# Layer C: two of the three channel slots run ahead of the gate's projection on TensorE

## What is computed

```python
h = rms_norm(x, rms_g)
z, xbc, dt = _split(h @ w_in, SPLIT_C)                 # gate, channels, steps
xbc, new_conv = causal_conv(xbc, conv_state, conv_w, conv_b)
xs, Bm, Cm = _split(silu(xbc), ...)
y, S = ssd_scan(xs, Bm, Cm, dt, A, S0)                 # chunked scan with a carried state
y = y + d_skip * xs
y = rms_norm(y * silu(z), g_y)                         # per group of 512
return x + y @ w_out
```

## Time and profile before

| | before |
|---|---|
| median of 3 runs (lowest, highest) | 2977.31 us (2972.36, 2978.59) |
| the profiled execution | 2970.96 us, its span 2969.1 us |
| TensorE matmul busy | 2774.0 us, 93% |
| TensorE weight load busy | 2313.0 us, 78% |
| VectorE busy | 1768.1 us, 60% |
| ScalarE busy | 1306.0 us, 44% |
| mean granted clock of TensorE | 0.966 |
| DMA | 324.89 MB, 109 GB/s over the span |

### The profile page before, as it was taken

One profiled execution on the slowest core, in us unless ns is written; L12 is line 12 of the kernel. 1 busy time (PEld: TensorE's weight loads), 2 busy tenths in 40 slices (PEclk: granted clock), 3 DMA queues, 4 the chain that ended last, 5 costly groups with the idle time before them and its releaser, 6 DMA issues. The chain is left out here.

```text
span 2969.1 us, 44869 instructions
## 1 busy us (share of the span) xinstructions
PE 2774.0 (93%) x16154; PEld 2313.0 (78%) x16154; DVE 1768.1 (60%) x4144; ACT 1306.0 (44%) x2635; POOL 45.6 (2%) x165
## 2 busy tenths in 40 slices
PE   6999997899999995799999999899999999599999
PEld 3788986577777774688877888688877888478787
DVE  3344443545555553588887888878887888632322
ACT  4455554534444442355454445544454544411211
POOL 0000000100000000000000000000000000000000
PEclk9999999999999997899999999899999999799999
DMA  5222222423233223633344333333343332244343
GB/s 187 88 91 90 76 76 75 136 92 113 105 116 116 106 90 104 174 91 93 93 122 113 100 100 104 123 112 100 99 122 117 100 99 72 86 167 145 133 143 105
DMA packets 281128, 324.89 MB, mean 109 GB/s; under 512 B 52807, under 2 KB 208970, under 8 KB 276778
## 3 DMA queue, kind: packets, MB, share of 16 engines
q1 hardware_dynamic: 279010, 317.77, 33.8%
q10 hardware_dynamic: 1992, 5.48, 0.5%
HBM read 238.89 MB, written 84.30 MB: 109 GB/s over the span
## 5 line engine op out<-in xcount | busy, mean ns | idle before, releaser
L2157 PE MATMUL bank<-h_high,wx_high 128*128 128x256 f32 (+1 forms) x1536 | 463.1, 301 | 2.3 <-DVE wx_low L2067 2.1
L2157 PE MATMUL bank<-h_high,wx_low 128*128 128x256 f32 (+1 forms) x1536 | 438.0, 285 | 0.0
L2157 PE MATMUL bank<-h_low,wx_high 128*128 128x256 f32 (+1 forms) x1536 | 437.2, 285 | 0.0
L2157 PEld LDWEIGHTS bank<-h_high,wx_high 128*128 128x128 f32 x1536 | 293.6, 191 | 24.5 <-issue 17.1
L2157 PEld LDWEIGHTS bank<-h_high,wx_low 128*128 128x128 f32 x1536 | 293.4, 191 | 17.2 <-issue 14.7
L2157 PEld LDWEIGHTS bank<-h_low,wx_high 128*128 128x128 f32 x1536 | 292.6, 191 | 0.0
L1978 DVE SCALAR_TENSOR_TENSOR conv_acc<-u,convw,conv_acc 128x256 f32<-128x256 f32 (+1 forms) x576 | 246.9, 483 | 13.4 <-ACT conv_acc L1860 11.1
L2148 PE MATMUL bank<-wz_high,h_high 128*128 128x512 f32 (+1 forms) x544 | 224.8, 413 | 5.4 <-DVE wz_low L2072 4.6
L2409 PE MATMUL bank<-wout_high,yT_high 128*128 128x512 f32 (+1 forms) x544 | 213.0, 392 | 6.5 <-DVE wout_low L2378 6.5
L2148 PE MATMUL bank<-wz_low,h_high 128*128 128x512 f32 (+1 forms) x544 | 216.3, 398 | 0.0
L2148 PE MATMUL bank<-wz_high,h_low 128*128 128x512 f32 (+1 forms) x544 | 216.2, 397 | 0.0
(11 more groups left out here) (294 smaller groups left out, 6141.7 us busy)
## 6 DMA issues: line engine op xcount, KB each, us to landing
h_high<-h1T_high_d SPq DMA_DIRECT2D x64, 512.0 KB, 6.1
h_low<-h1T_low_d SPq DMA_DIRECT2D x64, 512.0 KB, 7.0
acb<-acT SPq DMA_DIRECT2D x64, 512.0 KB, 3.8
yT_in<-yT SPq DMA_DIRECT2D x32, 1024.0 KB, 5.1
yT<-yT_t SPq DMA_DIRECT2D x64, 256.0 KB, 3.5
xin<-in_x_prompt SPq DMA_DIRECT2D x16, 512.0 KB, 3.6
h0T_high_d<-hT_high SPq DMA_DIRECT2D x16, 512.0 KB, 2.7
h0T_low_d<-hT_low SPq DMA_DIRECT2D x16, 512.0 KB, 3.5
```

Of the source, the lines that this page charges most:

```text
L2157: ins = M(out, wt[:, k, col:col + P], y[h.par][:, k, h.h0:h.h0 + h.n], start=(k == 0 and p == 0), stop=(k == KT - 1 and p == 2))
```

## The change

The two calls at the head of TensorE's step change places: slots 0 and 1 of the half come first, the gate's projection second. No instruction is added, removed or altered, and no other engine's program changes. In the functions `start` and in steps in which no half is due (the sample's, and units 15 and 16 of the last group) the order stays.

```diff
                 h = nxt.half if nxt is not None and not cur.sample else None
+                if h is not None:
+                    channels(h, cur, 0)
                 if nxt is not None:
                     gate(nxt, cur)
-                if h is not None:
-                    channels(h, cur, 0)
 
                 pe.wait_ge(s["st_new"], cur.st_before)
```

## The result

Six runs of the changed kernel gave a median of 2998.84 us (2991.61 to 3006.16), six of the kernel before 2976.63 us (2969.18 to 2978.59). The ratio is 1.0081, with a 95% interval of 1.0060 to 1.0102: the change makes the kernel slower, by 18 to 30 us. The profiled execution took 3001.40 us, its span 2999.5; against the profiled execution of before that is +30.4 us. That execution of before lay low in its runs and this one lies somewhat above its median, so the traces show 8 us more between them than the medians do.

A forecast was written before the change was run, and what follows sets the result against it. TensorE, busy 93% of the span, was taken as the bound, so time is won or lost where it waits. Terms -9.4 + 14 + 1 + 9 + 14 = +28.6 us, laid on the median, gave 3006 us, range 2979 to 3037.

The forecast's parts named there:

- The gain at the gate: TensorE no longer waits for zs at the gate; the whole excess of 52 units goes, -9.4 us.
- the 52 like units: Units 2 to 14 of each group, 987.5 us together, forecast to fall to 52 x 18.81 = 978.1 us.
- Even units 2 to 12: Late dtk stalls L2227 by 0.7 us in units 4 to 12, +14 us; unit 2 adds +1.
- T: Moment at which TensorE can start the next step: 0.85 us after the start of the state's update.
- VectorE's 2.1 us to spare: In even units, idle time with which VectorE can take back part of the decays' 2.8 us delay.
- the 12.4 us: Typical time from an odd unit's first load to dtk's landing, taken as set by the transfers.
- Rival B: Loads don't matter: VectorE's spare time swallows the delay or transfers land early; 2962 to 2968 us; chance 0.10.
- Unit 14: Unit 13's two more tiles' parts delay dtk; a stall of 3.1 us, 3 x 3 = +9 us.
- rival D: Stalls in units 14 and 16 and paced slots of unit 15 halve the clock: +70 to +85 us; chance 0.07.
- Change of group: In units 15 and 16, late gate weights make unit 16 end 4.6 us later, three times: +14 us.
- the piece that I had put into the range: In unit 15, slots paced by wx_low bring the clock down; second slot and gate pay 2 to 3 us.
- The sum of the terms: Whole kernel: -9.4 + 14 + 1 + 9 + 14 = +28.6 us; end to end +6 to +60.

The follow-up runs named there:

- the run with acb ahead: Changed kernel, but in odd units 1 to 13 SyncE issues store, acb and dtk before the wait for z_full and the pair's loads; 2980.42 us, ratio 1.0020.

## Why the prediction was right

The forecast was 3006 us with 2979 to 3037 around it, on a base of 2977.31; measured were 2998.84. Point by point:

- **The gain at the gate**, -9.4 us: with the loads out of the way the 52 like units fell from 987.5 to 977.8 us, -9.7. Right, and it is all of it: 18.8 us is TensorE's own work in a unit. The reading that 40.9 us of a weight load's idle time are worth 9.4 on TensorE was the step that mattered most on this side.
- **Even units 2 to 12**, forecast +15 with unit 2: the changed kernel has 11.2 us more there than the run with acb ahead, 10.9 of them in units 4 to 12. Landing was forecast at 11.8 to 13.3 us behind the first load; 24 sets of four loads gave 11.1 to 12.8, the three sets of six in unit 13 gave 13.9, 15.0 and 14.9. Decays started at T + 3.7 to 5.6, forecast 4 to 6. VectorE's 2.1 us to spare held: in units 4 to 12 the decays were 2.6 us late on average and the units 0.55 longer.
- **Luck in that landing.** I took the 12.4 us for the time of the transfers, which moves along with the first load. In the kernel before it was not: there the store's wait for VectorE set the issue of dtk, at T + 14.3 on average in units 3 to 11, 8.3 behind the first load, and dtk took 4.4. In the changed kernel the loads set it, at T + 18.6, 7.1 behind the first load, and dtk took 5.1. The two changes nearly cancel, 12.7 against 12.1. Of the 4.9 us by which dtk lands later, 4.3 are a later issue.
- **The order of landing.** dtk landed 1.6 to 3.2 us behind the last load in all 27, never ahead of it. The Trainium skill, page "DMA: Bandwidth & Descriptors", section "Queues, rings and completion order", has both halves, ring order and completion that is not first-in-first-out. These landings do not contradict the first, but they hardly test it: dtk was also issued 6.5 to 9.9 us behind the first load. Rival B fell with the measured time and with these landings; what held dtk up was chiefly that SyncE issues in order.
- **Unit 14**, forecast +9: 11.2. The three units grew by 3.1, 4.9 and 3.2 us where 3.1 was worked out, but not all of that is the wait: TensorE waited at L2187 and L2227 for 1.9, 2.9 and 2.7 us. In groups 0 and 1 the clock went down after it: from the start of L2227 to the next T took 3.7 and 4.3 us in place of 2.6. That is the term of the sum that was too small, by 2 us, for a clock that I had put into rival D alone.
- **Change of group**, forecast +14: unit 16 +18.6, unit 15 -3.8, together +14.8. Unit 16 was forecast to grow by 6 and grew by 5.2, 6.7 and 6.7. Unit 15 was forecast at 25.4 and took 27.0, 25.8 and 25.6. Here the piece that I had put into the range was real in part: the clock did go down in unit 15 (below). It cancels against another miss, and that is luck: I had worked from the shortest of the three units 15 of before, 26.8 us; the others took 27.4 and 28.1, and all three had a stretch at 1.2 GHz. The idle time of unit 16 stood at L2187 and not at L2227, as I had it; the amount was VectorE's delay all the same.
- **The sum of the terms** was +28.6 against +29.3 in layer C between the two traces. The measured 22 to 24 us between medians is less; two executions of one kernel differ by up to 15 us, which covers the difference but does not explain it. That the sum agrees so closely is luck in part: the even units were forecast 4 us too high and unit 14 2 us too low, and the term of the even units alone had 2 to 32. The ends of the sum, +6 and +60, are not what the bounds given for its terms add up to either, which is +9 and +54.

## What to carry to other kernels

When work on the bound engine is moved, look for what its semaphore releases in the DMA queue, and what stands behind that transfer: here a wait worth 9 us was removed, and 18 us (22 between the traces) went to loads that got in front of two transfers wanted sooner, another 15 to weights that came late. A queue that is issued in order should have what is wanted next ahead of a wait for buffers that are wanted two units later; with that, the same swap gains 0.4%. Where the engines have time to spare such a cost has a threshold, so half the move can keep all the gain; where they have none, as at the change of group, half the move still costs.

## What the runs showed of the hardware that I had not expected

**TensorE's clock fell twice around the turn from unit 14 to unit 15.** Windows of the changed kernel at the end of unit 14 and in unit 15 of group 0 (busy time of each engine, PEclk is the granted clock):

```profile
1512.00:1513.60 1.60, 0.82 (x7) 0.82 (x8) 1.60 (x3) 1.60 (x3) 0.00 (x0) 1.00 0.76 243
1513.60:1517.00 3.40, 3.40 (x14) 2.33 (x12) 2.30 (x4) 3.40 (x6) 0.00 (x0) 0.51 0.00 0
...
1517.00:1521.00 4.00, 1.76 (x8) 0.94 (x7) 3.61 (x5) 3.64 (x6) 0.00 (x0) 0.93 0.00 0
1521.00:1527.00 6.00, 6.00 (x21) 5.05 (x22) 5.97 (x11) 0.00 (x0) 0.00 (x0) 0.50 0.00 0
1527.00:1531.00 4.00, 4.00 (x28) 3.82 (x28) 3.65 (x18) 2.57 (x8) 0.00 (x0) 0.96 0.01 4
```

The granted clock is the third number from the end, ahead of the DMA share and the GB/s: 1.00, 0.51, 0.93, 0.50, 0.96. In unit 14 TensorE had just waited 1.92 us more at L2227; it went on at 2.4 GHz and 0.8 us later fell to 1.2; back at 2.4, it fell again after 4 us in which TensorE was busy for 1.76 (it idled 1.80 us in one piece for the first block of wx_low, then 0.21 and 0.23), and stayed down for 6 us of matmuls that no longer had to wait. Slots 0 and 1 ended at T + 13.6 in place of the T + 12.0 worked out.

Such a stretch does not always bring the clock down. In the run with acb ahead the same slots wait for the same blocks, and these are the windows of its unit 15 in group 0 (two) and group 2 (two):

```profile
1516.00:1520.00 4.00, 2.23 (x10) 1.44 (x10) 4.00 (x6) 4.00 (x6) 0.00 (x0) 0.91 0.00 0
1520.00:1524.00 4.00, 3.73 (x14) 2.94 (x15) 4.00 (x7) 2.61 (x4) 0.00 (x0) 0.66 0.00 0
```

```profile
2200.80:2204.80 4.00, 2.11 (x10) 1.44 (x11) 4.00 (x6) 4.00 (x6) 0.00 (x0) 1.00 0.00 0
2204.80:2208.80 4.00, 2.91 (x15) 2.00 (x16) 4.00 (x7) 2.50 (x4) 0.00 (x0) 1.00 0.00 0
```

In group 0 the clock fell, in group 2 it stayed at 2.4 GHz, and both units took 25.45 us. So a short stretch at the lower clock can cost nothing there, and what decides whether it comes stays open.

**An issue right behind loads takes longer.** SyncE took 0.36 us to issue the store in quiet units. Right behind four loads it took 1.75 us (above), and 1.3 to 2.2 in units 3 to 11 of all groups. In the run with acb ahead the third of four loads took 1.4 to 4.0 us, where it took 0.7 to 1.4 before the change. In unit 3 of group 1 before the change the store was issued 2.7 us after the last load's issue ended and took 0.38. That the transfers still under way are the reason is not shown.
